# One gate projection moved into the second hyena convolution, in two PSUM banks of its own

## The chip, the core and the metric

The kernel runs on one core of one Trainium2 chip. The metric is the device time of one execution in microseconds. Three runs of the kernel before took 2698.96, 2702.61 and 2702.1 us, with a median of 2702.1 us. The engines are called PE (TensorE, matrix multiplication), DVE (VectorE), ACT (ScalarE), POOL (GpSimd) and SP (SyncE, which here issues the weight loads).

## The reference, cut to what matters

A first block of two layers (a gated-linear-attention and state-space mixer with a dense and with a mixture-of-experts feed-forward) is followed by a second block. Its token mixer adds a hyena branch and an attention branch, each under its own gate; then comes PEER, a lookup of rows in a large table. The change touches only the token mixer:

```python
def token_mixer(h, p, attend):
    z = h @ p['w_in'] + p['b_in']
    q = rmsnorm_2(z[..., COL_Q:COL_K]...)          # COL_Q = 1536, COL_K = 2048
    ...
    y_hy = hyena(z[..., COL_HY:COL_Q], p) @ p['w_hy_out']
    y_na = attend(q, k, v).reshape(B, L, D_NA) @ p['w_na_out']
    gate = jax.nn.sigmoid(z[..., COL_G_HY:N_PROJ])  # columns 3072 to 5119
    merged = gate[..., :D_MODEL] * y_hy + gate[..., D_MODEL:] * y_na
    return merged @ p['w_out']
```

There are 256 tokens of 1024 channels. `hyena` does two long convolutions one after the other, each as a transform, a product with a filter spectrum and a transform back. The attention has 8 heads over 256 local and 256 context keys.

## The kernel before, in words

The program is written by hand, one instruction stream for each engine, joined by semaphores. Everything lies transposed, with channels on partitions. The order of the work is the order in which the code of each engine is written. PSUM has 8 banks; `bank(name, among)` gives the next one of a rotation and waits until whoever held it before has been read (`ps.free`). Each different `among` has a rotation of its own, but all share the record of who holds which bank.

In the stage "second" the order on PE is:

1. The rest of the first part: norms, the filters, and *pieces*. A piece is a generator (`piece`, `piece_tm`, `branch`) that multiplies one 512-column block of a weight by the tokens; `fill(n)` runs the next `n` pieces of the list `pieces` to their end, so that PE has work while DVE or ACT is busy. One `piece` gives 256 gate channels in two halves of 8 matmuls each, and ends at a `yield` after each half.
2. The loop `for o in range(2)` (line 1171): for each of the two convolutions transposes (`ytm`), forward transforms (`yre`, `yim`), a wait for the spectrum from DVE (line 1869 makes it), and the transforms back (`conv`).
3. `hyena done`. From here the buffer of the filters is dead. The gates are kept in that same memory (`m.filt, m.gate = filt, v4(filt, 16)`), so ACT may write no gate before `hyena done`.
4. For q, k and kc (the context keys): sums of squares (`qksum`, line 1207), one piece with `fill(1)`, the spreading of the root (`qknorm`, line 1218), and for q and k the rotary step (`rope`, line 1226). One more `fill(1)` comes behind them.
5. The attention loop of 16 iterations (head, half of the tokens). Iteration i has the transpose of the weights (`turn`, line 628), the scores of iteration i+3 (lines 1236 and 1237), one half of a piece with `next(halves, None)`, and the weighted sum (`attended`, line 620 with 64x128). Iteration 0 has a half ahead of `turn` as well, and iterations 3 and 4 have two.
6. `w_na`, then `w_out2`, the residual, and the stage "peer".

The gate pieces are named by their column: 3072, 3584, 4096 and 4608, two pieces each. `w_hy` is the output projection of the hyena branch, four pieces with 4 matmuls in each half. Before, 3072 (both), 3584 (first) and `w_hy` (0, 0) are the four `fill`s of item 4, and all others are halves in the attention loop, the last one in iteration 12.

On the side of ACT, `biased` copies a gate piece with its bias out of PSUM into `m.gate`, and `hy(i)` copies a `w_hy` piece. In the attention loop ACT does for each i: the exponential of iteration i+1 (`weights`), the copy of `turn` i, the context scores of i+2, one `hy` or `fill`, and the copy of `attended` i. DVE does the masked maximum of i+2 (`peak`, lines 1912 to 1916), the scaling of i+1 (`scaled`, lines 1921 and 1922), and then as many adaLN dot products (line 1416) as the tuple of the loop says: `(0, 0, 0, 0, 2, 2, 1, 1, 2, 2, 2, 2, 3, 1, 0, 0)`. These dot products belong to weights that SP loads into the same ring of slots as the gate weights, strictly in its own order.

Of the kernel before, what the change touches and what calls it, by code (L numbers as in the profile page):

```python
# [163 lines left out]
HALF = (4, 5, 6, 7)  # L164
WORK = (5, 6, 7)
ASIDE = (2, 3, 6, 7)
NOWN = 7

# [15 lines left out]
ROWS = row_places()  # L185
NROWS = NOWN + 10

# [8 lines left out]
def program(nc, T):  # L196
    with ExitStack() as ctx:  # L197
# [26 lines left out]
        hT = hflat.rearrange("p (k t) -> p k t", k=8)  # L224
# [385 lines left out]
        def pe(e):  # L610
            def bank(name, among=range(8)):
                b = ps.place(name, among)
                if ps.free(name):
                    e.wait_ge(*ps.free(name))
                return b
# [7 lines left out]
            def turned(b, ins):  # L623

                at = 0
                for x in ins:
                    k, m = x.shape
                    last = e.transpose(b[0:m, at:at + k], x, ident[0:k, 0:k])
                    at += k
                return last  # L630
# [431 lines left out]
            b = bank("final")  # L1062
# [9 lines left out]
            b = bank("norm_x")  # L1072
# [9 lines left out]
            def fill(n=1):  # L1082

                for _ in range(min(n, len(pieces))):
                    for _ in pieces.pop(0):
                        pass

            def piece(c0, i, n, rhs, ready):

                if i == 0:  # L1090
                    arrived(("w_in2", c0))
                tile = cols_of(("w_in2", c0))
                b = bank(("p2", c0, i))
                for j in range(2):
                    c = 128 * (2 * (i % 2) + j)
                    last = summed_as(half(b, j), [(tile[:, k, c:c + 128], rhs[:, k, :]) for k in range(8)], ready)
                    if j:
                        P.mark(last, ("p2", c0, i))
                        if i == n - 1:
                            done(("w_in2", c0))  # L1100
                    yield
# [29 lines left out]
            pieces = [piece(c0, i, 2, hT, "hT x") for c0 in (0, 512, 1024, 1536) for i in range(2)]  # L1131
# [5 lines left out]
            for i, (wname, rows) in enumerate((("f1w", 33), ("f2w", 64), ("f3w", 64))):  # L1137
                b = bank(("sin", i))
# [9 lines left out]
            for o in range(2):  # L1148
                for dr in range(2):
                    for t in range(2):  # L1150
                        b = bank(("f4", o, dr, t))
                        e.wait_ge(*A["sin", 2])
                        c0 = 1024 * o + 512 * dr
# [5 lines left out]
                b = bank(("abs", o))  # L1159
# [4 lines left out]
                for k in range(2):  # L1164
                    s = slice(128 * k, 128 * k + 128)
                    for what, mat, x in (("re", m.DC, 0), ("im", m.DS, 2)):
                        b = bank(("filter", o, k, what))
                        P.mark(summed(b, [(mat[:, t, s], m.fb[x + t]) for t in range(2)]), ("filter", o, k, what))
            for _ in range(3):
                fill(1)  # L1170
            for o in range(2):
                e.wait_ge(*V["conv in", o])
                for t in range(2):
                    b = bank(("ytm", o, t))
                    P.mark(turned(b, [m.zc[:, c, 128 * t:128 * t + 128] for c in range(4)]), ("ytm", o, t))
                for k in range(2):
                    s = slice(128 * k, 128 * k + 128)
                    br = bank(("yre", o, k))
                    e.wait_ge(*V["ytm", o, 1])
                    P.mark(summed(br, [(m.DC[:, t, s], m.y_tm[t]) for t in range(2)]), ("yre", o, k))  # L1180
                    bi = bank(("yim", o, k))
                    P.mark(summed(bi, [(m.DS[:, t, s], m.y_tm[t]) for t in range(2)]), ("yim", o, k))
                    fill(1)
                fill(1)
                e.wait_ge(*V["spectrum", o, 1])
                for c in range(4):
                    s = slice(128 * c, 128 * c + 128)
                    b = bank(("conv", o, c))
                    P.mark(summed(b[:, 0:256], [(m.yre[:, k, s], m.DCI[:, k, :]) for k in range(2)]
                                    + [(m.yim[:, k, s], m.DSI[:, k, :]) for k in range(2)]), ("conv", o, c))  # L1190
            fill(len(pieces))
            P.at["hyena done"] = P.now

            e.wait_ge(*V["hyena done"])
            e.wait_ge(*A["hyena done"])
            pieces = [piece(c0, i, 2, hT, "hT x") for c0, i in ((3072, 0), (3072, 1), (3584, 0))]
            pieces.append(branch("w_hy", m.zc, 0, 0))
            pieces.append(piece(3584, 1, 2, hT, "hT x"))
            pieces += [branch("w_hy", m.zc, n, p) for n, p in ((0, 1), (1, 0), (1, 1))]
            pieces += [piece(c0, i, 2, hT, "hT x") for c0 in (4096, 4608) for i in range(2)]  # L1200
            for x in ("q", "k", "kc"):
                b = bank(("qksum", x))
# [9 lines left out]
                for p in range(2):  # L1212
                    b = bank(("qknorm", x, p))
# [8 lines left out]
                if x != "kc":  # L1222
                    for p in range(2):
                        b = bank(("rope", x, p))
# [17 lines left out]
            for i, (h, t) in enumerate(its):  # L1242
                if i == 0:
                    next(halves)
                b = bank(("turn", i))
# [7 lines left out]
                b = bank(("attended", i))  # L1253
# [75 lines left out]
            for i in range(256):  # L1329
                t = i // 128  # L1330
# [731 lines left out]
        def act(e):  # L2062
            def a(out, src, func, name=None, **kw):
                A.mark(e.activation(out, src, func, **kw), name)  # L2064
                e.wait_ge(*A.now)
# [10 lines left out]
            def root(name, src, n, out):  # L2076

                e.wait_ge(*P[name])
                a(out, src, ACT.Sqrt, ("root", name), scale=1.0 / n, bias=eps)
# [32 lines left out]
            n = CS["ones"][0] + 128  # L2112
# [225 lines left out]
            def fill():  # L2338
                if pieces:
                    pieces.pop(0)()  # L2340
# [15 lines left out]
            pieces = [biased(512 * n, i, m.zh[:, 4 * n:4 * n + 4, 1:257], 4 * n) for n in range(3) for i in range(2)]  # L2356
# [25 lines left out]
            def hy(i):  # L2382
                a(m.hy[i], taken(("w_hy", i // 2, i % 2)), ACT.Copy, ("hy", i))
                emptied(("w_hy", i // 2, i % 2))
            pieces = [biased(3072 + 512 * n, i, m.gate[:, 4 * n:4 * n + 4, :], 24 + 4 * n)
                      for n in range(4) for i in range(2)]
            for x, xx in (("q", m.qn), ("k", m.kn), ("kc", m.kc)):
                a(m.sq, xx, ACT.Square, ("qksq", x))
                root(("qksum", x), ps.bank["qksum", x][:, 0:16], 64, m.r16[x])
                emptied(("qksum", x))  # L2390
                fill()
# [7 lines left out]
            def context_score(i):  # L2399
                a(m.sc[i % 2][:, 256:512], taken(("score", i))[:, 256:512], ACT.Copy, ("context score", i), scale=0.125)  # L2400
# [8 lines left out]
            context_score(0)  # L2409
            weights(0)  # L2410
            context_score(1)
            for i in range(16):
                h, t = divmod(i, 2)
                if i + 1 < 16:
                    weights(i + 1)
                a(m.pt[i % 2], taken(("turn", i)), ACT.Copy, ("turn", i))
                emptied(("turn", i))
                if i + 2 < 16:
                    context_score(i + 2)
                if i < 5 and i != 1:  # L2420
                    hy(max(i - 1, 0))
                elif i == 1 or i % 2 == 0:
                    fill()
                r = slice(64 * (h % 2), 64 * (h % 2) + 64)
                a(m.yna[r, h // 2, 128 * t:128 * t + 128], taken(("attended", i))[r, 0:128], ACT.Copy, ("attended", i))
                emptied(("attended", i))
# [276 lines left out]
```

## Time and profile before

| | us |
|---|---|
| median of three runs | 2702.1 |
| the profiled execution, whole | 2704.44 |
| its span, first to last instruction | 2702.5 |
| PE busy | 2506.6 (93%) |
| DVE busy | 2072.8 (77%) |
| ACT busy | 1257.6 (47%) |

### The profile page before, as it was taken

The page shows a single profiled execution, that of the slowest core. Times are in us where ns is not written, and L with a number is a line of the kernel's source. Part 1 is how long each engine was busy: PE and PEld are TensorE (multiplying, and loading weights), DVE is VectorE, ACT ScalarE, POOL GpSimd, SP SyncE. Part 2 cuts the span into 40 slices and gives each one's busy share as a digit, 9 for nine tenths or more (in the row PEclk, how much of TensorE's full clock was granted, in tenths as well). Part 3 has the DMA queues.
Part 4 walks back from the last instruction along what each step waited for, and adds up shares of the span by engine and source line. Part 5 has one row for each costly group of instructions (what it writes and reads, how often), then busy time and mean ns, then how long its engine had stood idle before and what let it go on. Part 6 is the DMA issues. An engine that isn't in the chain of part 4 may idle for free. (4 is left out here: it accounts for less than half of the span.)

```text
span 2702.5 us, 37397 instructions
## 1 busy us (share of the span) xinstructions
PE 2506.6 (93%) x14282; PEld 2161.1 (80%) x14282; DVE 2072.8 (77%) x3104; ACT 1257.6 (47%) x1540; POOL 271.6 (10%) x290
## 2 busy tenths in 40 slices
PE   5999999999999999999999999989998998778787
PEld 4789997787888888888888877747777898777786
DVE  6778984767898989899898974635748878887875
ACT  3234443236777777677777763103422333323322
POOL 0000001000000000000000000000003444333331
PEclk9999999989999999999999998999989999999999
DMA  8647675557999999999999956211558999999997
GB/s 350 245 176 285 273 286 199 216 197 286 354 356 355 356 346 344 355 353 356 353 358 354 355 190 240 114 42 67 212 236 347 412 421 420 420 421 421 421 421 298
DMA packets 109273, 824.90 MB, mean 305 GB/s; under 512 B 11864, under 2 KB 15192, under 8 KB 16096
## 3 DMA queue, kind: packets, MB, share of 16 engines
q1 hardware_dynamic: 71504, 551.75, 53.5%
q0 software_dynamic: 36864, 268.45, 24.0%
q8 instruction: 115, 1.88, 0.3%
q10 hardware_dynamic: 720, 2.24, 0.2%
q14 instruction: 70, 0.57, 0.1%
HBM read 821.34 MB, written 1.05 MB: 304 GB/s over the span
## 5 line engine op out<-in xcount | busy, mean ns | idle before, releaser
L1682 DVE TENSOR_TENSOR ring_r<-ring,arena_r 128x2048 fp32r<-128x2048 f32 x336 | 770.2, 2292 | 11.5
L2064 ACT ACTIVATE arena_r<-ring 128x2048 fp32r<-128x2048 f32 x378 | 725.6, 1920 | 29.0 <-DMA ring<-in_ffn_w_down 14.4
L634 PE MATMUL ps<-arena_r 128*128 128x512 f32 (+1 forms) x1120 | 417.2, 373 | 1.5 <-DVE arena_r L1718 1.5
L636 PE MATMUL ps<-arena_r 128*128 128x512 f32 x896 | 349.3, 390 | 0.0
L635 PE MATMUL ps<-ring_r,arena_r 128*128 128x512 f32 x896 | 348.6, 389 | 0.0
L1344 PE MATMUL ps<-sel,ring 128*128 128x128 f32 x2096 | 267.9, 285 | 59.7 <-ACT sel L2064 58.5
L1344 PEld LDWEIGHTS ps<-sel,ring 128*128 128x128 f32 x2096 | 251.9, 198 | 73.8 <-ACT sel L2064 71.5
L2064 ACT ACTIVATE sel<-cs,arena 128x128 f32<-128x128 f32 x256 | 102.8, 402 | 420.8 <-DVE arena L2022 381.5
L1344 PE MATMUL ps<-sel,arena 128*128 128x128 f32 x2000 | 249.5, 281 | 43.8 <-ACT sel L2064 38.1
L1344 PEld LDWEIGHTS ps<-sel,arena 128*128 128x128 f32 x2000 | 236.4, 195 | 55.3 <-ACT sel L2064 48.4
L634 PEld LDWEIGHTS ps<-arena_r 128*128 128x128 f32 x1120 | 211.3, 189 | 35.6 <-DVE arena_r L1718 1.8
L2064 ACT ACTIVATE arena<-ps 128x512 f32<-128x512 f32 (+2 forms) x210 | 106.0, 505 | 256.6 <-PE ps L620 103.6
L636 PEld LDWEIGHTS ps<-arena_r 128*128 128x128 f32 x896 | 168.2, 188 | 35.7
L635 PEld LDWEIGHTS ps<-ring_r,arena_r 128*128 128x128 f32 x896 | 168.4, 188 | 34.2
L2044 DVE CUSTOM_DVE_ANT_0 accb<-ring,ps 128x1024 f32<-128x1024 f32 x131 | 159.9, 1221 | 43.7 <-DMA ring<-in_uv,arena 36.8
L635 PE MATMUL ps<-arena_r 128*128 128x256 f32 x672 | 192.4, 286 | 0.0
L2044 DVE CUSTOM_DVE_ANT_0 accb<-arena,ps 128x1024 f32<-128x1024 f32 x125 | 152.6, 1221 | 40.4 <-DMA arena<-in_uv,arena 34.3
L634 PE MATMUL ps<-arena_r,h_r 128*128 128x512 f32 x448 | 178.4, 398 | 3.0 <-DVE ring_r L1682 1.7
L636 PE MATMUL ps<-arena_r,h_r 128*128 128x512 f32 x448 | 175.2, 391 | 0.0
L635 PE MATMUL ps<-ring_r,h_r 128*128 128x512 f32 x448 | 174.8, 390 | 0.0
L2064 ACT ACTIVATE arena<-arena 128x1 f32<-128x1 f32 (+6 forms) x366 | 115.3, 315 | 90.8 <-DVE arena L1875 18.2
L698 PE MATMUL ps<-h,ring 128*128 128x256 f32 (+1 forms) x608 | 144.7, 398 | 9.8 <-ACT h L2064 5.5
(282 smaller groups left out, 3864.0 us busy)
## 6 DMA issues: line engine op xcount, KB each, us to landing
ring<-in_moe_w_gate SPq DMA_DIRECT2D x112, 1024.0 KB, 5.4
ring<-in_moe_w_up SPq DMA_DIRECT2D x112, 1024.0 KB, 5.5
ring<-in_moe_w_down SPq DMA_DIRECT2D x112, 1024.0 KB, 5.2
ring<-in_ada_w SPq DMA_DIRECT2D x24, 1024.0 KB, 9.6
ring<-in_ada_w SPq DMA_DIRECT2D x12, 2048.0 KB, 7.9
ring<-in_w_in SPq DMA_DIRECT2D x10, 2048.0 KB, 10.5
ring<-in_w_ada SPq DMA_DIRECT2D x8, 2048.0 KB, 10.1
ring<-in_ffn_w_gate SPq DMA_DIRECT2D x14, 1024.0 KB, 5.2
```

The lines of the kernel that those rows point to most:

```text
L634: e.matmul(out, xs[0], ws[0], start=start, stop=False, skip_group_check=True)
L635: e.matmul(out, xs[0], ws[1], start=False, stop=False, skip_group_check=True)
L636: return e.matmul(out, xs[1], ws[0], start=False, stop=stop, skip_group_check=True)
L698: last = e.matmul(out, a, b, start=(i == 0), stop=(i == len(pairs) - 1))
L1344: last = e.matmul(ps.banks[2 * t + c // 4][:, 128 * (c % 4):128 * (c % 4) + 128], rows[:, 1024 + 128 * c:1152 + 128 * c], m.diag[:, i % ND ...
L1682: v(e.tensor_tensor(ring_low[ring.half[unit]], ring.buf[unit], mo.high[unit_at[unit] % NHIGH].bitcast(F32), ALU.subtract), ("low", unit))
L2044: v(e.tensor_tensor_reduce(m.waste, row_buffer(i)[0][:, 0:1024], x, 1.0, 0.0, ALU.mult, ALU.add, m.dots[:, i:i + 1]), ("dots", i))
L2064: A.mark(e.activation(out, src, func, **kw), name)
```

## The change

The first gate projection, columns 3072 to 3583, is taken out of `fill` and put as four halves into the second convolution: one half ahead of its forward transforms, one ahead of its wait for the spectrum, and two behind `hyena done`'s mark on PE. Its two results stay in banks 0 and 1 (`HELD`) until ACT may write the gates; the convolution uses the other six (`REST`). The four `fill`s behind it then run the two pieces of 3584 and the first two of `w_hy`. ACT takes the first held piece ahead of the root of q, and its `hy` and `fill` calls in the attention loop stand at other iterations.

```diff
+HELD = (0, 1)
+REST = (2, 3, 4, 5, 6, 7)
...
-            def piece(c0, i, n, rhs, ready):
+            def piece(c0, i, n, rhs, ready, among=range(8)):
...
-                b = bank(("p2", c0, i))
+                b = bank(("p2", c0, i), among)
...
+            gates = chain.from_iterable(piece(3072, i, 2, hT, "hT x", HELD) for i in range(2))
             for o in range(2):
+                among = REST if o else range(8)
                 e.wait_ge(*V["conv in", o])
                 for t in range(2):
-                    b = bank(("ytm", o, t))
+                    b = bank(("ytm", o, t), among)
...
+                if o:
+                    next(gates)
                 for k in range(2):
...
-                    br = bank(("yre", o, k))
+                    br = bank(("yre", o, k), among)
...
                 fill(1)
+                if o:
+                    next(gates)
                 e.wait_ge(*V["spectrum", o, 1])
...
             P.at["hyena done"] = P.now
+            next(gates)
+            next(gates)
...
-            pieces = [piece(c0, i, 2, hT, "hT x") for c0, i in ((3072, 0), (3072, 1), (3584, 0))]
+            pieces = [piece(3584, i, 2, hT, "hT x") for i in range(2)]
             pieces.append(branch("w_hy", m.zc, 0, 0))
-            pieces.append(piece(3584, 1, 2, hT, "hT x"))
...
                 a(m.sq, xx, ACT.Square, ("qksq", x))
+                if x == "q":
+                    fill()
                 root(("qksum", x), ps.bank["qksum", x][:, 0:16], 64, m.r16[x])
...
             context_score(1)
+            hy(0)
...
-                if i < 5 and i != 1:
-                    hy(max(i - 1, 0))
-                elif i == 1 or i % 2 == 0:
+                if i in (0, 1, 3):
+                    hy(i + 1 - i // 3)
+                elif i in (4, 5, 7, 9):
                     fill()
```

PE, from the transposes of the second convolution (128x128) to the sums of squares of q (128x2). `h,ring` with 128x256 is a gate piece, 8 matmuls to a half. Before:

```order
L628 MATMUL ps<-cs,arena 128x128 x8
L620 MATMUL ps<-arena 128x512 x4
L620 MATMUL ps<-ring,arena 128x512 x8
L620 MATMUL ps<-pv,cs 128x512
L620 MATMUL ps<-arena 128x512 x4
L620 MATMUL ps<-arena 128x256 x16
L1207 MATMUL ps<-cs,arena 128x2 x8
```

And now:

```order
L630 MATMUL ps<-cs,arena 128x128 x8
L700 MATMUL ps<-h,ring 128x256 x8
L622 MATMUL ps<-arena 128x512 x4
L622 MATMUL ps<-ring,arena 128x512 x8
L622 MATMUL ps<-pv,cs 128x512
L622 MATMUL ps<-arena 128x512 x4
L700 MATMUL ps<-h,ring 128x256 x8
L622 MATMUL ps<-arena 128x256 x16
L700 MATMUL ps<-h,ring 128x256 x16
L1216 MATMUL ps<-cs,arena 128x2 x8
```

Four halves (8, 8 and 16 matmuls) stand in the convolution or right behind it. The line numbers moved by the lines that were added.

PE, iteration 3 of the attention loop and the first instruction of iteration 4. `arena,ring` with 128x256 is `w_hy`. Before:

```order
L628 MATMUL ps<-cs,arena 128x128 x4
L1236 MATMUL ps<-arena 128x256
L1237 MATMUL ps<-arena 128x256
L620 MATMUL ps<-arena,ring 128x256 x8
L620 MATMUL ps<-arena 64x128 x4
```

And now:

```order
L630 MATMUL ps<-cs,arena 128x128 x4
L1245 MATMUL ps<-arena 128x256
L1246 MATMUL ps<-arena 128x256
L700 MATMUL ps<-h,ring 128x256 x16
L622 MATMUL ps<-arena 64x128 x4
```

Iterations 3 and 4 each carry two gate halves (16 matmuls) where they carried two `w_hy` halves (8 matmuls).

PE, iterations 9 to 12 of the same loop, of which one stands here. Before:

```order
L628 MATMUL ps<-cs,arena 128x128 x4
L1236 MATMUL ps<-arena 128x256
L1237 MATMUL ps<-arena 128x256
L698 MATMUL ps<-h,ring 128x256 x8
L620 MATMUL ps<-arena 64x128 x4
```

And now:

```order
L630 MATMUL ps<-cs,arena 128x128 x4
L1245 MATMUL ps<-arena 128x256
L1246 MATMUL ps<-arena 128x256
L622 MATMUL ps<-arena 64x128 x4
```

The gate half is gone from these four iterations.

## Rows read from the trace of the kernel before

**Rows 1.** Windows by stage; columns as in the header, PEclk is the granted clock.
```profile
core 0: us, PE busy (x) PEld busy (x) DVE busy (x) ACT busy (x) POOL busy (x), PEclk, DMA share, GB/s
1793.00:2016.00 223.00, 201.88 (x1014) 162.51 (x1014) 120.11 (x222) 63.07 (x127) 6.15 (x4) 0.94 0.41 165
2020.00:2700.00 680.00, 571.48 (x4452) 540.05 (x4450) 531.60 (x1451) 209.12 (x578) 240.37 (x256) 0.97 0.96 397
```

**Rows 2.** Timeline of PE: start, duration, instruction, and idle time before it.
```profile
1785.09 7.17 PE L620 MATMUL ps<-arena 128*128 128x256 f32 x32
1793.37 1.09 PE L628 MATMUL ps<-cs,arena 128*128 128x128 f32 x8 [1.10 <-DVE arena L1875]
1795.70 3.67 PE L620 MATMUL ps<-arena 128*128 128x512 f32 x8 [1.23 <-DVE arena L1857]
...
1815.40 9.58 PE L620 MATMUL ps<-arena 128*128 128x256 f32 x32 [4.49 <-DVE arena L1869]
1827.35 3.54 PE L1207 MATMUL ps<-cs,arena 128*128 128x2 f32 x16 [2.37 <-ACT arena L2064]
1830.75 8.73 PE L698 MATMUL ps<-h,ring 128*128 128x256 f32 x32
1839.41 1.97 PE L1218 MATMUL ps<-cs,arena 128*64 128x128 f32 x32
...
1844.18 1.84 PE L1207 MATMUL ps<-cs,arena 128*128 128x2 f32 x16
...
1859.44 7.15 PE L698 MATMUL ps<-h,ring 128*128 128x256 f32 x32
1866.53 1.97 PE L1218 MATMUL ps<-cs,arena 128*64 128x128 f32 x32
1868.42 3.72 PE L620 MATMUL ps<-arena,ring 128*128 128x256 f32 x16
1873.12 0.67 PE L1236 MATMUL ps<-arena 128*128 128x256 f32 x2 [0.97 <-issue]
```

**Rows 3.** Windows of short stretches, same columns as rows 1.
```profile
1813.60:1820.20 6.60, 4.80 (x11) 3.87 (x12) 2.55 (x5) 0.00 (x0) 0.00 (x0) 0.50 0.02 7
1827.30:1833.90 6.60, 6.55 (x24) 5.95 (x25) 1.22 (x2) 1.56 (x2) 2.49 (x2) 0.50 0.00 0
...
1953.00:1960.20 7.20, 3.50 (x25) 2.53 (x24) 6.88 (x13) 4.10 (x10) 0.00 (x0) 1.00 0.82 314
1961.00:1967.00 6.00, 4.92 (x20) 3.82 (x20) 5.82 (x10) 1.01 (x3) 0.00 (x0) 0.50 1.02 433
```

**Rows 4.** Timeline of PE in the attention loop.
```profile
1879.61 0.63 PE L628 MATMUL ps<-cs,arena 128*128 128x128 f32 x4 [0.21 <-DVE arena L1922]
...
1885.67 0.63 PE L628 MATMUL ps<-cs,arena 128*128 128x128 f32 x4
...
1887.00 1.89 PE L620 MATMUL ps<-arena,ring 128*128 128x256 f32 x8
...
1930.27 0.66 PE L628 MATMUL ps<-cs,arena 128*128 128x128 f32 x4
...
1931.63 3.61 PE L698 MATMUL ps<-h,ring 128*128 128x256 f32 x16
...
1954.16 0.66 PE L628 MATMUL ps<-cs,arena 128*128 128x128 f32 x4
...
1959.53 0.63 PE L628 MATMUL ps<-cs,arena 128*128 128x128 f32 x4 [2.25 <-DVE arena L1922]
...
1967.18 15.70 PE L620 MATMUL ps<-arena,ring 128*128 128x256 f32 x64 [0.42 <-ACT arena L2064]
```

**Rows 5.** Timeline of DVE in the attention loop, the scaling of four iterations.
```profile
1941.71 0.49 DVE L1922 TENSOR_SCALAR arena<-arena 128x512 f32<-128x512 f32 x1
...
1946.74 0.49 DVE L1922 TENSOR_SCALAR arena<-arena 128x512 f32<-128x512 f32 x1
...
1952.53 0.49 DVE L1922 TENSOR_SCALAR arena<-arena 128x512 f32<-128x512 f32 x1
...
1958.89 0.49 DVE L1922 TENSOR_SCALAR arena<-arena 128x512 f32<-128x512 f32 x1
```

**Rows 6.** Timeline of SP, the loads issued while the gate weights are in use.
```profile
1884.59 0.33 SPq L502 DMA_DIRECT2D ring<-in_w_in  x1
...
1905.71 0.33 SPq L502 DMA_DIRECT2D ring<-in_w_in  x1
1929.35 24.22 SPq L502 DMA_DIRECT2D ring<-in_w_ada  x4
```

More of the change, by code:

```diff
@@ L1170, in pe @@
                 fill(1)
+            gates = chain.from_iterable(piece(3072, i, 2, hT, "hT x", HELD) for i in range(2))
             for o in range(2):
+                among = REST if o else range(8)
                 e.wait_ge(*V["conv in", o])
                 for t in range(2):
-                    b = bank(("ytm", o, t))
+                    b = bank(("ytm", o, t), among)
                     P.mark(turned(b, [m.zc[:, c, 128 * t:128 * t + 128] for c in range(4)]), ("ytm", o, t))
+                if o:
+                    next(gates)
                 for k in range(2):
                     s = slice(128 * k, 128 * k + 128)
-                    br = bank(("yre", o, k))
+                    br = bank(("yre", o, k), among)
                     e.wait_ge(*V["ytm", o, 1])
                     P.mark(summed(br, [(m.DC[:, t, s], m.y_tm[t]) for t in range(2)]), ("yre", o, k))
-                    bi = bank(("yim", o, k))
+                    bi = bank(("yim", o, k), among)
                     P.mark(summed(bi, [(m.DS[:, t, s], m.y_tm[t]) for t in range(2)]), ("yim", o, k))
@@ L1187, in pe @@
                     s = slice(128 * c, 128 * c + 128)
-                    b = bank(("conv", o, c))
+                    b = bank(("conv", o, c), among)
                     P.mark(summed(b[:, 0:256], [(m.yre[:, k, s], m.DCI[:, k, :]) for k in range(2)]
```

## The prediction

> **What bounds the kernel now.** I read the busy shares by stage first, then the timelines of PE, DVE, ACT and SP between 1785 and 1970 us, then short windows for the clock. In the stage the change touches, 1793 to 2016 us, PE is busy 201.88 of 223 us and the DMA share is only 0.41; the stage behind it, 2020 to 2700 us, has a DMA share of 0.96 and starts only when this one has ended [rows 1]. So the bound here is PE, and a microsecond won or lost on PE's path to `w_na` goes through to the end. What PE waits for must be read place by place.
>
> In the second convolution PE waits 1.23 us ahead of the forward transforms, 4.49 us for the spectrum and 2.37 us for ACT's squares [rows 2]. After the last two it does not run at full speed: the granted clock is 0.50, that is 1.2 GHz, from 1813.6 to 1820.2 us and from 1827.3 to 1833.9 us [rows 3]. The attention loop has three regimes. Its start is set by DVE and ACT (`turn` 0 waits for the scaling), its middle by PE without a gap, and from `turn` 14 on again by DVE, with a wait of 2.25 us [rows 4].
>
> **Part 1, the convolution up to `qknorm` of q.** A gate half costs 3.55 us (half of the 7.15 us of a whole piece, 3.61 us with its last drain) [rows 2, 4].
> - The first half starts where the transposes end, 1795.70 - 1.23 = 1794.47, and ends at 1798.0. The transforms start 2.3 us later than before.
> - The second half lies inside the spectrum wait: 4.49 - 3.55 leaves 0.94 us idle, and the back transforms start at 1815.40 + 2.3 = 1817.7. After gaps of 1.10 and 1.23 us the engine kept its speed here (4 matmuls of 128x512 in 3.67 us), so I take it that they run in the 7.17 us of the first convolution and not in 9.58 [rows 2]: they are out at 1824.8.
> - The two halves behind them end at 1831.9. ACT's squares were ready 2.4 us after the back transforms ended, so the sums of squares of q no longer wait. They take 1.8 us (as k's) and not 3.54, and the piece behind them 7.1 and not 8.73 [rows 2]. `qknorm` of q starts at 1840.7, against 1839.41: **+1.3 us**, with 14.2 us of gate work done. The other 12.9 us are paid by 1.23 + 3.55 + 2.37 = 7.15 us of waits and by 2.4 + 1.7 + 1.6 = 5.7 us that the half clock had cost.
> - The new bank waits cost nothing here. Bank 0 was left by the first convolution's third result and bank 1 by its fourth, both read by DVE before the transposes start at 1793.37. ACT empties both held banks while PE is at q: the first right after the squares of q, the second behind its root, and the next users are `rope` of q and `qksum` of k.
>
> **Part 2, from q to the first scores.** q and k keep a whole gate piece each. kc has a `w_hy` piece of 3.7 us where it had 7.15, and the path there is PE's (DVE waits for it): -3.55. The first scores start at 1873.12 + 1.3 - 3.55 = 1870.9, **-2.2 us**.
>
> **Part 3, the start of the attention loop.** Ahead of `turn` 0 and in iteration 0 the halves are now `w_hy` ones (1.8 instead of 3.6 us). This gives nothing. `turn` 0 waited for DVE already (0.21 us), and `turn` 1 came 0.14 us behind the scaling that follows a chain of maximum, exponential, copy, context scores and maximum. PE just waits some 2 us ahead of `turn` 0 and again in iteration 0. `hy(0)` now stands ahead of `turn` 0, since it empties its bank; it runs beside the next maximum. I leave it at nothing up to iteration 3: **-2.2 us**.
>
> **Part 4, iterations 3 to 8.** Iterations 3 and 4 carry two gate halves where they had two `w_hy` halves: twice 2 x (3.55 - 1.8), **+7.0 us**, all of it on PE since nothing there waits for anyone else. 5 to 8 are as before. `turn` 9 comes at 1930.27 - 2.2 + 7.0 = 1935.1, **+4.8 us**.
>
> **Part 5, iterations 9 to 13.** This decides. Four halves of 3.55 us leave, 14.2 us. But the period there can't fall from 5.97 us (1930.27 to 1954.16 is four) [rows 4] to 2.4. DVE's own chain takes over: with two dot products to an iteration, from one scaling to the next is 1946.74 - 1941.71 = 5.03 us, and DVE has no gap in it [rows 5]. The tuple gives 2 dot products to the intervals 9 to 12, so four periods are 20.1 us and not 23.9: -3.8. `turn` 13 comes at 1954.16 - 3.8 + 4.8, +1.0. The next interval has three dot products, 1958.89 - 1952.53 = 6.36 us [rows 5]. Before, `turn` 13 was itself 1.1 us behind its scaling (1952.53 + 0.49 against 1954.16), since PE was late; now it isn't, so that slack is gone too: `turn` 14 and `w_na` are at **+2.1 us**. Of the 14.2 us that left, 2.7 were worth anything.
>
> **Loads.** PE frees 3584 some 30 us earlier and 4096 some 20 us earlier than before, so the loads of 4096 and 4608 and of the last adaLN weights go out earlier [rows 6], and none can come late. The adaLN load that DVE waited for near 1937 us (issued at 1929.35) is early now; that wait lay beside PE's work, so it gives nothing.
>
> The sum is -2.2 + 7.0 - 3.8 + 1.1 = **+2.1 us** against the profiled execution (whole 2704.44, span 2702.5). The median of the runs is 2.3 us below that execution; I add the difference to the median: **2704.2 us**.
>
> **The open sizes.** (a) The clock in the new gaps. The 2 us ahead of `turn` 0 are near the 2.37 us after which the clock was 0.50. At half clock PE's 4.2 us of iteration 0 become 8.4, against a period of 6.06 (1879.61 to 1885.67): up to +2.6 us; if the clock holds, 0. (b) In iterations 9 to 12 PE is busy half of the time, as in 1953.0 to 1960.2 (3.50 of 7.20 us), behind which the clock fell to 0.50 [rows 3]. At half clock PE needs 4.7 us of 5.03, so the period stands; only `w_na` may start slow for longer than now, up to 1.5 us. Below, where the clock should last through the end, 1.5 us (15.70 against 4 x 3.55) is won [rows 4]. (c) If the 0.94 us left ahead of the back transforms still lowers the clock, 2.4 us of the saving go. I take 0 for each, since the nearest rows (gaps of 1.0 to 1.2 us) kept 1.00.
>
> The Trainium skill (TensorE: Matmul & The Clock Gate, "A second HAM failure mode: psum-queue depth-cycling") warns that short idles between groups of matmuls that cycle through banks make the clock go down and up again, and that throughput suffers from it. By that rule the emptied iterations are a loss on their own, as rival B has it. The trace has such a stretch and agrees that the clock falls in it; it doesn't show that the period grows.
>
> **Rivals.**
> - *A, the halves are worth their full length.* If PE bounded iterations 9 to 12 throughout, 14.2 us would go and not 3.8, and the end would be at +2.1 - 10.4 = -8.3 us: **2694 us**. For it speaks that PE has no gap there now; against it that DVE's chain of 5.03 us runs without a gap too.
> - *B, slower: the clock.* The gap ahead of `turn` 0 lowers it (+2.6) and the sparse loop keeps it low into `w_na` (+1.5): +6.2, **2708.3 us**. It decides from the point where the gap of about 2 us is enough; 2.37 us was, 1.23 us wasn't.
> - *C, slower: the filling doesn't restore the clock in the convolution.* Then 5.7 us are missing: +7.8, **2709.9 us**. Against it: after the fill PE has no gap above 1 us there.
> - *D, it moves nothing:* the timed runs did not have the two slow-clock stretches that the profiled execution had (it is 2.3 us above their median). Then the saving is smaller by some of the 5.7 us; or the chains have slack that I don't see, and the end is at 0 to +4.
>
> **How the numbers follow.** My forecast (with D, both from about -1.5 to +4.5 us) has 0.72. B has 0.12, C 0.05, A 0.06, and 0.05 is for others. Of this kernel a measurement can't tell less than about 0.2%, 5.4 us, from no change. Slower by over that is most of B and C: 0.16. Faster by over that is A and a little: 0.08. Within it: 0.76. The range reaches from 2698.5 (-3.6) to 2709 (+6.9), as the open sizes lie above rather than below.
>
> **What would show it.** In the profile after: back transforms in about 7.2 us at clock 1.00 (part 1); `qksum` of q without a wait and at full speed; first scores near 1871 us; `turn` 9 near 1935 us (part 4); from `turn` 9 to 13 periods near 5.0 us with PE waiting for the scaling (part 5); `w_na` near 1969 us. The forecast is wrong if those periods are near 4 us or less, if `turn` 1 isn't 6 us behind `turn` 0, or if a gate half waits for its bank.

## The result: slower by 6.5 us, three times the forecast

| | kernel before | changed kernel |
|---|---|---|
| median of the timed runs, us | 2702.46 (17 runs) | 2708.97 (17 runs) |
| lowest to highest, us | 2694.61 to 2705.19 | 2704.94 to 2711.22 |
| profiled execution, whole / span, us | 2704.44 / 2702.5 | 2711.22 / 2709.4 |

The ratio is 1.0026, with a 95% interval of 1.0018 to 1.0033: the change costs 6.5 us, and at least 4.9. I had forecast +2.1 us, and had given 0.76 to a change too small to measure. The direction of the sum was right, its size was not. The measured 2708.97 us lies just inside the stated range, which ended at 2709; that is due to the width of the range and says nothing for the mechanism.

The first view of the changed kernel is PE's timeline through the second convolution up to `turn` 0, with start, duration, instruction and idle time before it. It answers to [rows 2] and the first row of [rows 4]. Line numbers lie up to 9 higher.

```profile
1797.08 1.09 PE L630 MATMUL ps<-cs,arena 128*128 128x128 f32 x8 [1.10 <-DVE arena L1884]
1798.01 3.62 PE L700 MATMUL ps<-h,ring 128*128 128x256 f32 x16
...
1816.45 3.62 PE L700 MATMUL ps<-h,ring 128*128 128x256 f32 x16
1821.10 7.17 PE L622 MATMUL ps<-arena 128*128 128x256 f32 x32 [1.04 <-DVE arena L1878]
1828.11 7.07 PE L700 MATMUL ps<-h,ring 128*128 128x256 f32 x32
1835.02 1.84 PE L1216 MATMUL ps<-cs,arena 128*128 128x2 f32 x16
1836.72 7.15 PE L700 MATMUL ps<-h,ring 128*128 128x256 f32 x32
...
1874.06 0.67 PE L1245 MATMUL ps<-arena 128*128 128x256 f32 x2 [0.97 <-issue]
...
1880.72 0.66 PE L630 MATMUL ps<-cs,arena 128*128 128x128 f32 x4 [2.10 <-ACT arena L2073]
```

The fills work as expected. The spectrum wait of 4.49 us is down to 1.04, the back transforms take 7.17 us and not 9.58, the sums of squares of q (L1216) wait for nothing, and the piece behind them takes 7.15 us and not 8.73. The clock during the back transforms is 1.00 in a window of them:

```profile
1821.00:1828.20 7.20, 7.10 (x33) 6.27 (x34) 2.77 (x7) 0.00 (x0) 0.00 (x0) 1.00 0.01 2
```

Before anything is subtracted, the start of this list needs care. The code ahead of the transposes (the first row) is the same in both kernels, yet they start at 1797.08 us here and at 1793.37 us in [rows 2]. Over the twelve profiles of this study, all with the same code up to that point, the start lies between 1793.37 and 1797.08 (mean 1794.9 for those with the changed order, 1795.1 for those with the order before). So 3.71 of the 6.87 us between the two profiled executions are chance, and I count every stage from its own start of the transposes:

| us from the start of the transposes | before | changed | difference | forecast |
|---|---|---|---|---|
| first scores | 79.75 | 76.98 | -2.77 | -2.2 |
| `turn` 9 | 136.90 | 141.05 | +4.15 | +4.8 |
| `w_na` | 173.81 | 175.56 | +1.75 | +2.1 |
| last matmul of `w_out2` | 216.86 | 218.59 | +1.73 | +2.1 |
| from there to the end of the span | 692.27 | 693.70 | +1.43 | 0 |

Up to `w_na` every step of the forecast is within 0.7 us. The attention loop, again PE's timeline, answers to [rows 4]; between 1905 and 1940 us `turn` has nothing to wait for, at both ends it has:

```profile
1886.62 0.63 PE L630 MATMUL ps<-cs,arena 128*128 128x128 f32 x4 [1.63 <-DVE arena L1931]
...
1895.71 0.63 PE L630 MATMUL ps<-cs,arena 128*128 128x128 f32 x4 [0.52 <-DVE arena L1931]
...
1905.06 0.66 PE L630 MATMUL ps<-cs,arena 128*128 128x128 f32 x4
...
1914.43 0.65 PE L630 MATMUL ps<-cs,arena 128*128 128x128 f32 x4
...
1938.13 0.66 PE L630 MATMUL ps<-cs,arena 128*128 128x128 f32 x4
...
1943.05 0.63 PE L630 MATMUL ps<-cs,arena 128*128 128x128 f32 x4 [1.80 <-DVE arena L1931]
...
1948.09 0.63 PE L630 MATMUL ps<-cs,arena 128*128 128x128 f32 x4 [2.51 <-DVE arena L1931]
...
1958.16 0.63 PE L630 MATMUL ps<-cs,arena 128*128 128x128 f32 x4 [2.51 <-DVE arena L1931]
...
1964.53 1.09 PE L630 MATMUL ps<-cs,arena 128*128 128x128 f32 x4 [2.96 <-DVE arena L1931]
...
1972.64 15.68 PE L622 MATMUL ps<-arena,ring 128*128 128x256 f32 x64 [0.42 <-ACT arena L2073]
```

Iterations 3 and 4 take 9.35 and 9.37 us (1895.71 to 1905.06 to 1914.43) where they took 5.9. From `turn` 9 on PE waits for DVE's scaling in every iteration and the period is 4.92, 5.04, 5.03, 5.04, then 6.37 us. DVE's timeline, the scalings, answers to [rows 5] with the same distances of 5.04 and 6.36 us:

```profile
1942.42 0.49 DVE L1931 TENSOR_SCALAR arena<-arena 128x512 f32<-128x512 f32 x1
...
1947.46 0.48 DVE L1931 TENSOR_SCALAR arena<-arena 128x512 f32<-128x512 f32 x1
...
1957.53 0.49 DVE L1931 TENSOR_SCALAR arena<-arena 128x512 f32<-128x512 f32 x1
...
1963.89 0.49 DVE L1931 TENSOR_SCALAR arena<-arena 128x512 f32<-128x512 f32 x1
```

The clock in the emptied iterations, in the columns of [rows 1]:

```profile
1938.00:1948.00 10.00, 5.23 (x34) 3.83 (x32) 8.63 (x19) 6.05 (x15) 0.00 (x0) 1.00 0.75 284
1948.00:1958.00 10.00, 6.67 (x32) 4.93 (x32) 9.55 (x18) 4.07 (x11) 0.00 (x0) 0.83 0.87 346
1960.00:1972.00 12.00, 7.36 (x32) 5.74 (x30) 11.51 (x22) 2.55 (x6) 0.00 (x0) 0.50 0.61 221
```

It falls to 0.83 and 0.50, as open size (b) had it, and the period of 5.03 us stands. By single iterations the clock is 1.00, 0.66, 1.00 and 0.55 (from 1943.05, 1948.09, 1953.12 and 1958.16 us on), with periods of 5.04, 5.03, 5.04 and 6.37 us. The loads are earlier as forecast: the two loads of gate weights go out at 1857.46 and 1894.25 us (in [rows 6] at 1884.59 and 1905.71), the adaLN load behind them at 1913.52 us (in [rows 6] at 1929.35). Counted from the transposes these are 30.8, 15.2 and 19.5 us.

```profile
1913.52 26.96 SPq L504 DMA_DIRECT2D ring<-in_w_ada  x4
```

So the stage that I argued about gave about what I said, and the rest is behind it. The start of the stage "peer" was in none of my rows. First the kernel before, PE's timeline at the last `norm_peer` spread (L686) and the first query (L1311), then the changed kernel at the same place:

```profile
2014.23 0.71 PE L686 MATMUL ps<-cs,arena 128*128 128x128 f32 x4 [0.68 <-DVE arena L1370]
...
2016.28 6.78 PE L1311 MATMUL ps<-h,ring 128*128 128x128 f32 x32 [1.33 <-ACT h L2064]
```

```profile
2019.67 0.71 PE L688 MATMUL ps<-cs,arena 128*128 128x128 f32 x4 [0.68 <-DVE arena L1379]
...
2024.69 6.59 PE L1320 MATMUL ps<-h,ring 128*128 128x128 f32 x32 [4.31 <-DVE h L1392]
```

And DVE in the changed kernel:

```profile
2020.49 4.10 DVE L1392 SCALAR_TENSOR_TENSOR h<-xT,arena,ps 128x256 f32<-128x256 f32 x8 [0.87 <-PE ps L688]
```

The first query starts 5.02 us behind the spread and not 2.05 us. It waits 4.31 us for DVE's eight multiplications (L1392), and not 1.33 us for ACT's rounding of the first of them. The reason is a bank. `norm_sums("norm_peer", range(8))` takes the next bank of the common rotation; the queries take theirs from a fixed list, `ASIDE = (2, 3, 6, 7)`, and the first query always gets bank 2. Before, the rotation stood at bank 6 when it came to `norm_peer`. The change takes twelve allocations out of the common rotation: ten of the second convolution (transposes, forward and back transforms) go to `REST`, the two gate pieces to `HELD`. Twelve steps less among eight banks lead from bank 6 to bank 2, and that is what `norm_peer` gets now. All eight multiplications read that bank, and the first query may only overwrite it when the last one has read it. Nothing in the stage "peer" was edited.

### The profile page after: what moved, and what is told of

The parts are those of the page before. It is cut to its first block and busy times, and to the rows that moved or that the text cites. A ratio compares the mean times of both kernels' runs of the same rounds, so it can differ in the third digit from the quotient of the medians.

```text
span 2709.4 us, 37397 instructions
## 1 busy us (share of the span) xinstructions
PE 2494.7 (92%) x14282; PEld 2149.9 (79%) x14282; DVE 2072.6 (76%) x3104; ACT 1257.6 (46%) x1540; POOL 271.1 (10%) x290
## 5 line engine op out<-in xcount | busy, mean ns | idle before, releaser
L1353 PE MATMUL ps<-sel,ring 128*128 128x128 f32 x2096 | 259.5, 280 | 65.4 <-ACT sel L2073 64.4
L1353 PEld LDWEIGHTS ps<-sel,ring 128*128 128x128 f32 x2096 | 244.4, 193 | 78.9 <-ACT sel L2073 76.7
## 6 DMA issues: line engine op xcount, KB each, us to landing
ring<-in_w_in SPq DMA_DIRECT2D x10, 2048.0 KB, 10.8
```

Source lines behind the costliest of these rows:

```text
L1353: last = e.matmul(ps.banks[2 * t + c // 4][:, 128 * (c % 4):128 * (c % 4) + 128], rows[:, 1024 + 128 * c:1152 + 128 * c], m.diag[:, i % ND ...
```

## The experiments

The first four vary the parts that I had argued about, on one chip; the next four test the bank and a better order, on another; the last two are on a third. Each chip has its own runs of the kernel before. In the short diffs "-" is the kernel that the experiment starts from.

**e1: the kernel before, with its two convolution waits filled by unread matmuls.** It takes the filling alone, with all else in place.

```diff
+                if o:
+                    arrived(("w_in2", 3072))
+                    busy(8, 3)          # 8 matmuls of 128x256 in bank 3
                 e.wait_ge(*V["spectrum", o, 1])
...
             P.at["hyena done"] = P.now
+            busy(5, 7)                  # 5 in bank 7
```

> The kernel before, with matmuls that nobody reads put into its two waits in the second convolution: 8 of 128x256 (3.55 us) into the spectrum wait of 4.49 us, 5 (2.2 us) into the wait of 2.37 us ahead of the sums of squares of q. Nothing else is moved. Theory 1 (the prediction's failed step is that it took the profiled execution's slow-clock stretches as always there): the stretches are as long as in the profile only in some executions, so the mean saving is less than 5.7 us, near 4 us: about 0.15% faster than the kernel before. Rival (they are there in full in every execution): 5.7 us, 0.21% faster. If it is 0 to 1 us the clock in these two places isn't worth anything in timed runs and the +6.5 us of the changed kernel must be explained elsewhere. Profile: back transforms in 7.2 us, squares' sums in 1.8 us, first scores about 5.7 us nearer to the transposes of the second convolution than the 79.75 us of before.

Measured: 2697.06 us (7 runs) against 2704.27 us (29 runs) of the kernel before, ratio 0.9971 (0.996 to 0.9983), 7.2 us faster. PE's timeline of e1:

```profile
1818.49 7.17 PE L620 MATMUL ps<-arena 128*128 128x256 f32 x32 [1.04 <-DVE arena L1878]
1825.50 2.32 PE L620 MATMUL ps<-h,ring 128*128 128x256 f32 x10
1828.03 1.92 PE L1216 MATMUL ps<-cs,arena 128*128 128x2 f32 x16 [0.21 <-ACT arena L2073]
1829.81 8.84 PE L698 MATMUL ps<-h,ring 128*128 128x256 f32 x32
```

Matmuls whose results nobody reads make the kernel faster, by 4.6 to 10.8 us by the interval. The 5.7 us that I had put on the half clock lie within it, and the 4 us of my first theory (slow stretches that stand in only some executions) lie just outside. The profile of e6 fits that: from the transposes to the sums of q it has 33.99 us, the kernel before 33.98. So the runs speak against the first half of rival D: the timed executions had slow stretches worth about what the profile shows. The profile of e1 itself gives less at this place, and here I missed: the first scores come 75.83 us behind the transposes where they came at 79.75, so 3.9 us are won and not 5.7. The clock fell once more, and the piece at 1829.81 takes 8.84 us and not 7.15. Another 2.4 us are won up to the end of `w_out2`, where nothing was edited: `w_na` takes 14.08 us and not 15.70, at a clock of 1.00. So where the clock is low does shift between executions in that part, and the 7.2 us are not all tied to the two waits.

**e2: the changed kernel with one half in every iteration.**

```diff
                 next(halves, None)
-                if 3 <= i < 5:
-                    next(halves, None)
...
-                if i in (0, 1, 3):
-                    hy(i + 1 - i // 3)
-                elif i in (4, 5, 7, 9):
+                if i in (0, 1, 2):
+                    hy(i + 1)
+                elif i in (4, 6, 8, 10):
                     fill()
```

> The changed kernel with one half in each iteration of the attention loop from 1 on, none doubled in 3 and 4, so that the last gate half stands in iteration 10 and not in 8 (ACT's copies are moved with them). Theory (iterations 9 and 10 have room for a half at a cost of 5.93 - 5.03 = 0.9 us each, since DVE's chain of 5.03 us sets them anyway, while 3 and 4 lose 3.55 us each): 7.1 - 1.8 = 5.3 us faster than the changed kernel, so about +1 us against the kernel before. Rival (PE's time is the sum that counts wherever a half stands): same as the changed kernel, +6.5. Profile: turn 3 to turn 5 in 11.9 us and not 18.7; turn 9 to 11 in 11.9 and not 10.0.

Measured: 2703.94 us (11 runs), ratio to before 0.9999 (0.999 to 1.0008), 4.1 us below the changed kernel of the same chip (2708.06 us, e4). From `turn` 0 to `turn` 14 it takes 78.68 us where the changed kernel takes 83.81, 5.1 less. PE's timeline around the place:

```profile
1905.78 0.66 PE L630 MATMUL ps<-cs,arena 128*128 128x128 f32 x4
1911.71 0.66 PE L630 MATMUL ps<-cs,arena 128*128 128x128 f32 x4
...
1941.32 0.66 PE L630 MATMUL ps<-cs,arena 128*128 128x128 f32 x4
1946.24 0.63 PE L630 MATMUL ps<-cs,arena 128*128 128x128 f32 x4 [1.80 <-DVE arena L1929]
```

The period stays at 5.92 us from iteration 3 on. The +7.0 us of my part 4 are gone, and what it gives back at the end is less, since the DVE-bound stretch begins two iterations later.

**e3: the changed kernel with DVE's dot products earlier, where PE is the bound.**

```diff
-            for i, dots in enumerate((0, 0, 0, 0, 2, 2, 1, 1, 2, 2, 2, 2, 3, 1, 0, 0)):
+            for i, dots in enumerate((0, 0, 4, 4, 0, 2, 2, 2, 2, 1, 1, 0, 0, 0, 0, 0)):
```

> The changed kernel with only the tuple of DVE's dot products changed, to (0, 0, 4, 4, 0, 2, 2, 2, 2, 1, 1, 0, ...): eight of them in the two long iterations, at most one in those without a half. Theory (DVE's chain, with its dot products, sets iterations 9 to 13): the periods there fall from 5.03 to 4.34 in three and from 6.36 to 4.34 in the one with three dot products, 4.1 us faster than the changed kernel, about +2.4 against the kernel before. Rival (the clock or PE sets them): no change against the changed kernel. A second way to miss: the adaLN weights that the earlier dot products want are still in flight, then DVE shows a wait on DMA of 1 to 5 us in iteration 5.

Measured: 2705.28 us (11 runs), ratio 1.0005 (0.9996 to 1.0014), 2.8 us below e4 (expected 4.1; the intervals of the two ratios overlap). From `turn` 0 to `turn` 14 the profile has 80.14 us and not 83.81. PE's timeline in its emptied iterations, and one maximum on DVE:

```profile
1941.20 0.77 PE L630 MATMUL ps<-cs,arena 128*128 128x128 f32 x4 [1.80 <-DVE arena L1931]
1945.68 0.63 PE L630 MATMUL ps<-cs,arena 128*128 128x128 f32 x4 [0.34 <-DVE arena L1931]
1950.19 0.63 PE L630 MATMUL ps<-cs,arena 128*128 128x128 f32 x4 [1.80 <-DVE arena L1931]
1954.52 0.63 PE L630 MATMUL ps<-cs,arena 128*128 128x128 f32 x4 [1.81 <-DVE arena L1931]
1958.86 1.09 PE L630 MATMUL ps<-cs,arena 128*128 128x128 f32 x4 [0.93 <-DVE arena L1931]
```

```profile
1952.03 0.42 DVE L1921 SCALAR_TENSOR_TENSOR arena<-ps,ring 128x256 f32<-128x256 f32 x1 [1.99 <-ACT arena L2073]
```

With one dot product or none in the interval the period is 4.3 to 4.5 us and not 5.03. With two or three, as in the changed kernel, the number of dot products on DVE sets the length, as part 5 said. Below that another limit takes over: DVE now has idle time of its own, 0.84 us with one dot product and 1.99 us with none, in which it waits for ACT. What is left is the round through three engines (PE's `turn`, ACT's copies, DVE's maximum and scaling), 4.33 us. It is still far from PE's 2.4 us, so rival A fails here too.

**e4: the changed kernel again, beside e1 to e3.** No edit.

> The changed kernel again, unchanged, on the same chip and in the same rounds as the three others. Expected: 1.0024 to 1.0029 of the kernel before. Its profile is a second execution: by theory 1 the slow-clock stretches fall elsewhere against the program, the part up to the convolution differs by 1 to 4 us from the first profile though its code is the same, and the changed stage, from the transposes of the second convolution to w_na, is again 175.6 us long within 1.5 us.

Measured: 2708.06 us (11 runs), ratio 1.0015 (1.0006 to 1.0024), +3.8 us. The loss is there, though smaller than in the first session; the two intervals overlap. Its profile puts `w_na` 175.55 us behind the transposes (175.56 in the first), although the transposes start 3.6 us earlier: the changed stage repeats, its start does not.

**e5: the changed kernel with `norm_peer` back in bank 6.**

```diff
-            norm_sums("norm_peer", range(8))
+            norm_sums("norm_peer", (6,))
```

> The changed kernel with one bank fixed: the sums of the peer stage's norm take bank 6, as in the kernel before, and not the rotation's next, which the change has moved to bank 2. Theory 2 (part of the slowdown is a new wait at the start of the peer stage: the first query's bank is always 2, and with the norm's sums there it waits for the last of DVE's eight scalings, 4.31 us idle where it was 1.33): 2.9 us faster than the changed kernel; against the kernel before +1 to +2.5 us, ratio 1.0004 to 1.0009. In the profile the idle time ahead of the first query is 1.33 us again, and from its norm's sums (128x1) to the first query 5.8 us and not 8.8. Rival (the longer slow clock at the peer stage's start comes by chance): no change, ratio 1.0015 to 1.0025, and the stretch from the last output projection to the end stays at 693.5 to 695 us.

**e6: the kernel before with `norm_peer` in bank 2.**

```diff
-            norm_sums("norm_peer", range(8))
+            norm_sums("norm_peer", (2,))
```

> The kernel before, with the sums of the peer stage's norm put into bank 2, nothing else. Theory 2: 2.9 us slower than the kernel before (ratio 1.0011), with an idle time of 4.31 us ahead of the first query. Rival: the same as the kernel before.

PE at the start of the peer stage, e5 and then e6:

```profile
2015.62 1.22 PE L688 MATMUL ps<-cs,arena 128*128 128x128 f32 x4 [0.68 <-DVE arena L1379]
...
2018.17 6.08 PE L1320 MATMUL ps<-h,ring 128*128 128x128 f32 x32 [1.33 <-ACT h L2073]
```

```profile
2016.55 0.71 PE L686 MATMUL ps<-cs,arena 128*128 128x128 f32 x4 [0.68 <-DVE arena L1370]
...
2021.57 6.58 PE L1311 MATMUL ps<-h,ring 128*128 128x128 f32 x32 [4.31 <-DVE h L1383]
```

Both ways the number of the bank alone switches the wait: 1.33 us for ACT with bank 6, 4.31 us for DVE with bank 2. Timed beside one kernel before (2703.5 us, 33 runs): e5 2706.0 us (11 runs), ratio 1.0011 (1.0002 to 1.002); e6 2706.24 us (11 runs), ratio 1.0008 (0.9999 to 1.0017). So the wait is shown, and its price less firmly: the bank alone costs 2.7 us as timed, with an interval that just touches none (-0.3 to +4.6 us), and the rest of the change costs 2.5 us. Together they make 5.2 us, between the two measurements of the whole change (+6.5 and +3.8). Over all profiles the time from `w_out2` to the end agrees: a mean of 693.8 us in the five with bank 2 (changed, e2, e3, e4, e6), and of 691.1 us in the seven others (691.5 without e8 and e10, which change the start of this stage). Single pairs scatter around that: e6 has only 0.4 us more there than the kernel before, e5 2.8 us less than the changed kernel and 4.0 less than e4.

**e7: a better order, first try.** It has e5's bank, one half in each iteration, the two halves of 4096 earlier in the list of pieces, and DVE's dot products from iteration 0 on.

```diff
-            pieces += [branch("w_hy", m.zc, n, p) for n, p in ((0, 1), (1, 0), (1, 1))]
-            pieces += [piece(c0, i, 2, hT, "hT x") for c0 in (4096, 4608) for i in range(2)]
+            pieces.append(branch("w_hy", m.zc, 0, 1))
+            pieces.append(piece(4096, 0, 2, hT, "hT x"))
+            pieces += [branch("w_hy", m.zc, 1, p) for p in range(2)]
+            pieces.append(piece(4096, 1, 2, hT, "hT x"))
+            pieces += [piece(4608, i, 2, hT, "hT x") for i in range(2)]
...
-                if 3 <= i < 5:
-                    next(halves, None)
...
+            for i, dots in enumerate((1, 1, 1, 1, 2, 2, 2, 2, 2, 2, 1, 1, 0, 0, 0, 0)):
...
+                if i in (0, 2, 4):
+                    hy(i // 2 + 1)
+                elif i in (1, 6, 8, 10):
                     fill()
```

> The changed kernel with what the runs so far point to: bank 6 for the norm's sums; the first piece of 4096 ahead of turn 0 and in iteration 0, where PE waited 2.1 and 1.6 us; w_hy halves in 1 to 4; one gate half in each of 5 to 10; DVE's dot products as (1, 1, 1, 1, 2, 2, 2, 2, 2, 2, 1, 1, 0, 0, 0, 0). Theory (DVE's and ACT's chain of 4.34 us sets an iteration without a gate half, PE's 5.93 us one with): turn 0 to turn 14 in 72 us and not 83.8; with the bank 14.7 us faster than the changed kernel, about 0.9963 of the kernel before. Rival (the clock falls in the sparse iterations and eats it): 0.998 or more, with turn 1 to 5 at 5 us and more each.

Measured: 2704.6 us (11 runs), ratio 0.9998 (0.9989 to 1.0007). This missed what I expected. DVE, then SP, then PE say why:

```profile
1923.29 1.28 DVE L1426 CUSTOM_DVE_ANT_0 sel<-ring,accb,pv 128x1024 f32<-128x1024 f32 x1 [9.11 <-DMA ring<-in_w_ada]
```

```profile
1914.40 32.84 SPq L504 DMA_DIRECT2D ring<-in_w_ada  x4
```

```profile
1915.32 0.66 PE L630 MATMUL ps<-cs,arena 128*128 128x128 f32 x4
...
1928.43 1.08 PE L630 MATMUL ps<-cs,arena 128*128 128x128 f32 x4 [7.12 <-DVE arena L1932]
```

A dot product waits 9.11 us for adaLN weights whose load SP could only issue at 1914.40, when PE had finished with 4096 and freed its slot. DVE reached it too early, its scaling stood behind the wait, and one iteration took 13.11 us.

**e8: e7 with unread matmuls in the sparse iterations and at the start of the peer stage.**

```diff
+            def busy(name, n):
+                b = bank(("busy", name))
+                summed(half(b, 0), [(ident, cs[:, 0:256]) for _ in range(n)])
...
+                if i > 9:
+                    busy(i, 3)
...
             norm_sums("norm_peer", (6,))
+            busy("sums", 1)
             spread("norm_peer")
+            busy("spread", 2)
```

> e7 with matmuls that nobody reads: three of 128x256 (1.3 us) behind the weighted sum in iterations 10 to 15, and one and two around the spreading of the peer stage's norm. Theory 1 (the clock's slow stretches cost where PE is on the path): the tail of the loop, w_na and the first query run at full speed, 2 to 4 us faster than e7. Rival (the extra matmuls are themselves in the way): the same as e7 or up to 3 us slower.

Measured: 2703.05 us (11 runs), ratio 0.9999 (0.999 to 1.0008). Both ratios stand at none, so the timing doesn't tell e8 from e7. In the profile the stretch from `turn` 14 to `w_out2` takes 21.46 us and not 23.39 us.

**e9: e7 with the dot products of the late weights put back behind their load.**

```diff
-            for i, dots in enumerate((1, 1, 1, 1, 2, 2, 2, 2, 2, 2, 1, 1, 0, 0, 0, 0)):
+            for i, dots in enumerate((1, 1, 1, 1, 2, 2, 0, 0, 2, 2, 1, 1, 1, 1, 0, 0)):
...
-            some(hidden, 5)
+            some(hidden, 7)
```

> e7 with DVE's dot products put where their weights have arrived: (1, 1, 1, 1, 2, 2, 0, 0, 2, 2, 1, 1, 1, 1, 0, 0) and two more behind the loop. In e7 the ninth one waited 9.1 us for a load that SP can issue only when the second piece of 4096 is done, in iteration 6. Theory (that wait was what ate e7's gain): no wait on a DMA in the loop, turn 0 to turn 14 in 72 us and not 82.7, e7's time less 9 to 10 us, 0.9962 to 0.9970 of the kernel before. Rival (the sparse iterations are slowed by the clock anyway): above 0.999.

Measured: 2696.86 us (8 runs) against 2704.16 us (12 runs), ratio 0.9972 (0.9961 to 0.9982), 7.3 us faster than before. The wait for the load is gone, and the iteration that took 13.11 us takes 5.93:

```profile
1921.16 0.66 PE L630 MATMUL ps<-cs,arena 128*128 128x128 f32 x4
...
1927.09 0.66 PE L630 MATMUL ps<-cs,arena 128*128 128x128 f32 x4
```

From `turn` 0 to `turn` 14 it takes 73.38 us, against 79.92 before and 83.81 in the changed kernel.

**e10: e9 with e8's unread matmuls.**

```diff
+                if i > 10:
+                    busy(i, 3)
...
+            busy("sums", 1)
             spread("norm_peer")
+            busy("spread", 2)
```

> e9 with the unread matmuls of e8 (three of 128x256 in iterations 11 to 15, one and two at the peer stage's norm). Theory 1: the slow-clock stretch over the tail of the loop and w_na goes (in e8's profile it did), 2 to 3 us faster than e9, about 0.9953 to 0.996 of the kernel before. Rival: the same as e9.

Measured: 2692.03 us (5 runs), ratio 0.996 (0.9946 to 0.9974), 12.1 us faster than before. The windows of the tail, e9 and then e10:

```profile
1948.00:1962.00 14.00, 9.95 (x39) 7.72 (x40) 12.85 (x23) 5.42 (x13) 0.00 (x0) 0.53 0.62 219
```

```profile
1940.00:1960.00 20.00, 16.73 (x92) 12.95 (x93) 17.91 (x33) 9.94 (x19) 0.00 (x0) 1.00 0.72 281
1960.00:1972.00 12.00, 12.00 (x58) 10.57 (x57) 8.48 (x14) 3.40 (x3) 0.00 (x0) 1.00 0.34 145
```

With three unread matmuls behind each `attended` of iterations 11 to 15 the clock stays at 1.00 through the tail and into `w_na`; without them it is 0.53 in the tail. From `turn` 14 to `w_out2` it takes 21.46 us against 22.96 us in e9. Timed, e10 lies 4.8 us below e9, but the intervals of the two ratios overlap, so the timing doesn't show that it is the faster of the two. Both are faster than the kernel before; the changed kernel was not timed beside them.

## Why the prediction was wrong, point by point

**The failed step** is the first paragraph's "a microsecond won or lost on PE's path to `w_na` goes through to the end". It took the stages behind as unchanged, and so gave them nothing. They held a new wait of 3.0 us (4.31 against 1.33), made by the change itself: the rotation of banks runs on from stage to stage, and the peer stage mixes it with a fixed list. Next to it stands the sentence "The new bank waits cost nothing here". I had asked who uses the two held banks next, inside the stage; the right question was which bank every later allocation gets now. e5 and e6 show the mechanism in both directions, with the waits at 1.33 and 4.31 us in either kernel; the timed cost of 2.7 us has an interval that touches none. In the two main profiles the part behind `w_out2`, forecast at 0, is 1.43 us longer.

- **Part 1, the convolution.** Right in mechanism: `qknorm` of q starts 46.73 us behind the transposes where it started at 46.04, +0.7 us for a forecast +1.3. e1 shows that filled waits pay by themselves: 7.2 us timed, of which its profile ties 3.9 to this place.
- **Part 2, first scores.** -2.77 for -2.2. Right.
- **Part 3, start of the loop.** `turn` 0 waits 2.10 us for ACT and `turn` 1 1.63 us for DVE, with 5.90 us between them (1880.72 to 1886.62). The long half had been free, and so was the short one. Open size (a) is 0: rival B's first part is out.
- **Part 4.** +4.15 at `turn` 9 for +4.8. Right, and e2 shows that the pair of halves in iterations 3 and 4 costs 5.1 us of the loop in the profile and 4.1 us as timed (expected 5.3).
- **Part 5.** Periods of 5.03 and 6.37 us for 5.03 and 6.36. Right; e3 shows that their length hangs on the dot products, down to a round of 4.33 us through ACT that I had not seen. Rival A (2694 us) is out for this order.
- **Open size (b).** The clock fell in the emptied iterations to 0.50 and `w_na` started slow, 15.68 us in all, as long as before (15.70). So the extra 1.5 us that rival B wanted didn't come, but the clock didn't last either. The Trainium skill (TensorE: Matmul & The Clock Gate, "A second HAM failure mode: psum-queue depth-cycling") says that short idles between groups of matmuls, in a loop that cycles through PSUM banks, make the clock swing and cost throughput. The trace agrees on the clock (0.83 and 0.50) and not on the period, which another engine sets (5.03 and 5.04 us).
- **Rival C.** Out: back transforms in 7.17 us at clock 1.00, the piece behind the sums in 7.15 us.
- **The sum.** The stage gave +1.75 us in the profile for +2.1, and +2.5 us as timed in e5 (0.5 to 5.4). The bank adds 2.7 to 3.0. That is 4.5 to 5.5 us, where two measurements of the whole gave 6.5 and 3.8. The lowest bound of the first is 4.9, so it is explained within its interval, but a remainder of 1 to 2 us in its middle is not tied to any row. It stays open.
- **The chances.** 0.16 for slower rested on rivals that are all about the clock. None of them is what happened. I had no rival for an effect outside the stage.

## What to carry to other kernels

A counter that hands out buffers in turn carries a change into stages that nobody edited: after moving an allocation, list which buffer each later user gets, and look where such a rotation meets a fixed list. Taking work from a stretch is worth only what is left until the next engine's chain (here 5.03 us of DVE against 2.4 of PE), so work goes from PE-bound iterations into idle ones and the other engine's work the opposite way, as e9 does, with each load's release checked against its new user (e7). The two waits of PE of 4.49 and 2.37 us cost twice here, once as idle time and once as half clock behind them, and in e1 matmuls that nobody reads paid for themselves in them.

## What the runs showed of the hardware that I had not expected

- Thirteen unread matmuls in two waits made a kernel of 2.7 ms 7.2 us faster (e1, 0.9971, 0.996 to 0.9983). The waits themselves were 4.49 and 2.37 us [rows 2].
- In e1 the piece behind the sums of 2 columns (128x2, 1.92 us) took 8.84 us, although PE shows as busy in the sums and the piece: the clock was still 1.00 in the sums and 0.59 in the first 4.2 us of the piece. With a whole piece ahead of the sums, as in the changed kernel, it took 7.15. Whether the narrow sums or the idle times of 1.04 and 0.21 us ahead of them let the clock fall is not shown.
- The same code up to the transposes ended 3.7 us apart between executions (1793.37 and 1797.08 us), half of the whole difference between the two profiles. Without counting from a common mark I would have looked for it in the change.
- A lower granted clock cost nothing where PE only waited for another engine: in the changed kernel an iteration took 5.04 us at 1.00 (1943.05 to 1948.09) and 5.03 us at 0.66 (1948.09 to 1953.12). The one with three dot products took 6.37 us at 0.55, and in the kernel before its scalings stood 6.36 us apart.
